# Hybrid decoder block with expert retrieval: both halves of the expert V rows accumulated by TensorE in two lasting PSUM banks

## The reference

```python
h = rmsnorm(x); q, k, v, gb, gc, hc = split(h @ w_in, 6)            # 6 parts of 512 columns
x = x + concat(rmsnorm(stick_breaking_attention(q, k, v)),           # 8 heads of 64
               rmsnorm(gb * conv3(gc * hc))) @ w_out
xn = rmsnorm(x)
# PEER, for each token and each of 8 heads:
s1, s2 = query halves @ keys            # 2 x 128 scores; top 16 of each, then top 16 of the 256 sums
idx, g = 16 expert numbers, softmax of their sums
act = gelu(dot(xn, u_tab[idx]))         # one dot product of 1024 per expert
x = x + sum over the 128 experts of (g * act) * v_tab[idx]
out = rmsnorm(x)
```

## Time and profile before

| | |
|---|---|
| runs | 3486.37, 3487.28, 3492.98 us; median 3487.28 us |
| profiled execution | 3507.52 us, its span 3505.8 us |
| TensorE busy with matmuls | 2478.2 us (71% of the span), 7568 |
| TensorE loading weights | 1334.6 us (38%) |
| VectorE busy | 2666.1 us (76%), 6520 |
| ScalarE, GpSimd busy | 691.0 us (20%), 1359.8 us (39%) |
| DMA | 1213.87 MB, mean 346 GB/s; gathers take 78.5% of 16 engines' span, plain loads and stores 10.4% |
| granted TensorE clock | 0.843 of full speed |
| chunk sums (L1355) start at | 689.3, 1147.6, 1591.2, 1985.8, 2378.9, 2772.3, 3133.3, 3495.1 us |

### The profile page before, as it was taken

How to read it: one execution, slowest core, us unless ns; L and a number is a source line. 1 busy time by engine, 2 the same in 40 slices (tenths; PEclk the granted TensorE clock), 3 DMA queues, 4 the chain that set the end, 5 groups by cost and what they waited for, 6 DMA issues and landing times.

```text
span 3505.8 us, 29116 instructions
## 1 busy us (share of the span) xinstructions
PE 2478.2 (71%) x7568; PEld 1334.6 (38%) x7568; DVE 2666.1 (76%) x6520; ACT 691.0 (20%) x1951; POOL 1359.8 (39%) x1296
## 2 busy tenths in 40 slices
PE   8569985589989785675878787676567555544554
PEld 7447463256545342223544333343223222211221
DVE  1674789865778799896778788689877577777776
ACT  2022311121434111112114332111111111111111
POOL 0132322333334333444444444344444444454443
PEclk9889998799999897898988898798888767776777
DMA  6878797789888997899998999999888899999997
GB/s 216 321 299 324 275 380 289 282 337 355 329 315 331 380 365 303 334 346 365 404 410 338 350 362 382 389 402 369 343 347 338 334 381 383 378 368 371 373 378 301
DMA packets 187117, 1213.87 MB, mean 346 GB/s; under 512 B 20704, under 2 KB 22752, under 8 KB 55520
## 3 DMA queue, kind: packets, MB, share of 16 engines
q0 software_dynamic: 147456, 1073.81, 78.5%
q1 hardware_dynamic: 39520, 138.45, 10.4%
HBM read 1198.54 MB, written 13.63 MB: 346 GB/s over the span
## 4 chain that ended last, share of the span: by engine, by line
PE 34%; DVE 30%; DMA 22%; issue 6%; ACT 5%; POOL 2%; POOLq 0%; DVEq 0%; ACTq 0%; SPq 0%
DMA ring<-in_uv,cur_idx 20%; PE vacc L922 16%; DVE ring L1103 12%; PE bank L960 7%; DVE acc L1134 4%; PE bank L1028 3%; ACT diag L747 3%; POOL ring L710 2%; PE o_ps L926 2%; DMA xn<-in_final_norm_g 1%; PE bank L956 1%; DVE lt L1251 1%; DVE ocT L1261 1%; PE bank L989 1%; PE bank L971 1%
## 5 line engine op out<-in xcount | busy, mean ns | idle before, releaser
L922 PE MATMUL vacc<-ring,diag 128*128 128x512 f32 x2048 | 1281.9, 771 | 968.8 <-ACT diag L747 964.9
L710 POOL DMA_INDIRECT ring<-in_uv,cur_idx x1024 | 1198.1, 1170 | 1191.9 <-PE vacc L922 661.9
L1103 DVE CUSTOM_DVE_ANT_0 ring<-ring,xn 128x1024 f32<-128x1024 f32 x1024 | 1221.0, 1223 | 367.8 <-DMA ring<-in_uv,cur_idx 361.1
L922 PEld LDWEIGHTS vacc<-ring,diag 128*128 128x128 f32 x2048 | 488.6, 250 | 1658.2 <-ACT diag L747 1005.2
L1134 DVE SCALAR_TENSOR_TENSOR acc<-ring,g_w,acc 128x512 f32<-128x512 f32 x832 | 625.6, 752 | 35.2 <-DVE g_w L1126 0.6
L701 POOL COPY cur_idx<-idx 128x4 uint32<-128x4 uint32 (+1 forms) x256 | 159.7, 624 | 924.5 <-DVE acc L1134 706.2
L742 ACT ACTIVATE g_ex<-g_cu 128x4 f32<-128x4 f32 x256 | 52.4, 205 | 2071.8 <-DVE g_cu L1116 2041.0
L747 ACT ACTIVATE diag<-ident,g_w 128x128 f32<-128x128 f32 x1024 | 326.9, 390 | 185.6 <-DVE g_w L1126 181.8
L960 PE MATMUL bank<-hT,wpool 128*128 128x256 f32 (+2 forms) x1280 | 285.3, 382 | 1.4 <-ACT hT L773 1.4
L960 PEld LDWEIGHTS bank<-hT,wpool 128*128 128x128 f32 x1280 | 220.1, 193 | 69.3 <-issue 12.3
L1039 PE MATMUL bank<-hT,wpool 128*128 128x256 f32 (+2 forms) x1024 | 234.2, 384 | 0.7 <-ACT hT L857 0.7
(11 more groups left out here) (129 smaller groups left out, 1813.8 us busy)
## 6 DMA issues: line engine op xcount, KB each, us to landing
wpool<-in_w_in SPq DMA_DIRECT2D x96, 512.0 KB
wpool<-in_peer_wq SPq DMA_DIRECT2D x64, 512.0 KB
wpool<-in_w_out SPq DMA_DIRECT2D x32, 512.0 KB
ring<-in_uv,cur_idx POOLq DMA_INDIRECT x1024, 8.6
xb<-in_x SPq DMA_DIRECT2D x15, 512.0 KB
x_scratch<-xb SPq DMA_DIRECT2D x8, 512.0 KB
xn_scratch<-xb SPq DMA_DIRECT2D x8, 512.0 KB
xn<-xn_scratch SPq DMA_DIRECT2D x8, 512.0 KB
```

What stands on the lines that cost most here:

```text
L710: nc.gpsimd.indirect_dma_start(ring[:, s, :], None, uv, bass.IndirectOffsetOnAxis(ap=cur_idx[:, s:s + 1], axis=0))\
L922: ins = nc.tensor.matmul(vacc[:, :], diag[:, q, s, :], ring[:, q * GROUP + s, D:D + PE_COLS], start=first and s == 0, stop=last and s == G ...
L1103: ins = nc.vector.tensor_tensor_reduce(out=ring[:, s, 0:D], in0=ring[:, s, 0:D], in1=xn[:, c % 2, :], scale=1.0, scalar=0.0, op0=ALU.mult, ...
```

## The change

Every group is now treated as the wide ones were, with a PSUM bank of its own for the second half. `wide_groups`, `is_wide`, `add_rows` and the semaphore `s_vd` are gone. The new bank `vacc2` is taken from the front stages: BANKS falls from 6 to 5. The pool "att" keeps four banks (1 to 4), "mix" has one (0) where it had two, and "all" has five. GpSimd waits for `s_vp` where it waited for `s_vd` before it copies the indices. `final_sum` always has two additions.

```diff
-BANKS = 6
+BANKS = 5
-            choice = {"all": range(BANKS), "att": range(2, BANKS), "mix": range(2)}[pool_of]
+            choice = {"all": range(BANKS), "att": range(1, BANKS), "mix": range(1)}[pool_of]
+        vacc2 = ctx.enter_context(nc.psum_tensor("vacc2", [P, D - PE_COLS], F32))
...
                 if not very_first:
-                    pool.wait_ge(s_vd, used + 1)
+                    pool.wait_ge(s_vp, used + 1)
                 nc.gpsimd.tensor_copy(cur_idx[:, sl], ...)
...
                     if not very_first:
-                        pool.wait_ge(s_vd, used + s % GROUP + 1)
                         pool.wait_ge(s_vp, used + s % GROUP + 1)
...
                 for s in range(GROUP):
-                    ins = nc.tensor.matmul(vacc[:, :], diag[:, q, s, :], ring[:, q * GROUP + s, D:D + PE_COLS], ...)
-                    if wide:
-                        ins = nc.tensor.matmul(o_ps[:, :], diag[:, q, s, :], ring[:, q * GROUP + s, D + PE_COLS:2 * D], ...)
-                    ins.then_inc(s_vp, 1)
+                    nc.tensor.matmul(vacc[:, :], diag[:, q, s, :], ring[:, q * GROUP + s, D:D + PE_COLS], ...)
+                    nc.tensor.matmul(vacc2[:, :], diag[:, q, s, :], ring[:, q * GROUP + s, D + PE_COLS:2 * D],
+                                     ...).then_inc(s_vp, 1)
...
                     weights(G, sl)
-                    if is_wide(c, i, q):
-                        dve.sem_inc(s_vd, GROUP)
-                    else:
-                        add_rows(c, G, q, first)
...
                     dve.wait_ge(s_vp, (c + 1) * SLOTS)
-                    dve.wait_ge(s_vd, (c + 1) * SLOTS)
-                    if c in wide_from:
-                        nc.vector.tensor_tensor(acc[:, c % 2, PE_COLS:D], o_ps[:, :], acc[:, c % 2, PE_COLS:D], ALU.add)
+                    nc.vector.tensor_tensor(acc[:, c % 2, PE_COLS:D], vacc2[:, :], acc[:, c % 2, PE_COLS:D], ALU.add)
```

More of the change, by code:

```diff
@@ L253, in timeline @@
     return out
[L256 to L264, removed]
 def batch_of(c):
@@ L315, in build @@
     line = timeline()
-    wide_from = wide_groups(line)
     phases = [("pe", "turn_keys"), ("act", "store_keys")] + [ph[1:] for ph in line if ph[0] == "front"]
@@ L505, in build @@
         s_gw = sem("s_gw")
-        s_vd = sem("s_vd")
         s_diag = sem("s_diag")
@@ L524, in span @@
             return slice(lc_of(c) * P, (lc_of(c) + 1) * P)
-        def is_wide(c, i, q):
-            return c in wide_from and 2 * i + q >= wide_from[c]
         def gather_line(eng_group, eng_front, me):
@@ L915, in group @@
                     pe.wait_ge(s_fsum, c)
[L916 to L919, removed]
                 pe.wait_ge(s_diag, n * 2 + q + 1)
                 for s in range(GROUP):
-                    ins = nc.tensor.matmul(vacc[:, :], diag[:, q, s, :], ring[:, q * GROUP + s, D:D + PE_COLS],
-                                           start=first and s == 0, stop=last and s == GROUP - 1,
-                                           skip_group_check=True)
-                    if wide:
-                        ins = nc.tensor.matmul(o_ps[:, :], diag[:, q, s, :], ring[:, q * GROUP + s, D + PE_COLS:2 * D],
-                                               start=first_wide and s == 0, stop=last and s == GROUP - 1,
-                                               skip_group_check=True)
-                    ins.then_inc(s_vp, 1)
+                    nc.tensor.matmul(vacc[:, :], diag[:, q, s, :], ring[:, q * GROUP + s, D:D + PE_COLS],
+                                     start=first and s == 0, stop=last and s == GROUP - 1, skip_group_check=True)
+                    nc.tensor.matmul(vacc2[:, :], diag[:, q, s, :], ring[:, q * GROUP + s, D + PE_COLS:2 * D],
+                                     start=first and s == 0, stop=last and s == GROUP - 1,
+                                     skip_group_check=True).then_inc(s_vp, 1)
             def front(name, args):
@@ L997, in front @@
                         pe.wait_ge(s_gain, c)
[L998 to L1002, removed]
                     for i in range(4):
@@ L1126, in weights @@
                 nc.vector.tensor_tensor(g_w[:, sl], g_xg[:, sl], g_re[:, sl], ALU.mult).then_inc(s_gw, 1)
[L1128 to L1136, removed]
             def front(name, args):
@@ L1350, in front @@
                     dve.wait_ge(s_vp, (c + 1) * SLOTS)
-                    dve.wait_ge(s_vd, (c + 1) * SLOTS)
-                    if c in wide_from:
-                        nc.vector.tensor_tensor(acc[:, c % 2, PE_COLS:D], o_ps[:, :], acc[:, c % 2, PE_COLS:D],
-                                                ALU.add)
+                    nc.vector.tensor_tensor(acc[:, c % 2, PE_COLS:D], vacc2[:, :], acc[:, c % 2, PE_COLS:D], ALU.add)
                     nc.vector.tensor_tensor(acc[:, c % 2, 0:PE_COLS], vacc[:, :], acc[:, c % 2, 0:PE_COLS], ALU.add)\
```

## The result

The changed kernel takes 3873.1 us (median of 4 runs, 3870.6 to 3879.3) against 3487.4: ratio 1.109, interval 1.107 to 1.111. It is 386 us slower where 212 were forecast, and lies outside the range. The profiled execution took 3871.3 us, its span 3869.6.

A forecast was written before the change was run, and what follows sets the result against it. No engine is full on average; TensorE, VectorE or DMA bounds it by stretch. Terms 141 - 34 + 30 + 50 + 15 + 10 = 212 us on the median 3487.3 gave about 3700 us, range 3590 to 3810.

The forecast's parts named there:

- three kinds of stretch: Core read in windows: TensorE full, VectorE full with TensorE half idle, or DMA nearly full (chunks 3, 4, 6, 7).
- The lost bank: In the "mix" pool each use waits until the one before was read: plus 50 us, bounds 0 and 100.
- the first wait: Second part of `out_proj(c, 0)` waits for VectorE's read of the first, over 23 group parts: 48 us.
- The tail: Chunks 6 and 7: two matmuls and the index copy delay the next gather: plus 15 us, bounds minus 15 and plus 95.
- The chain's own step: Chunks 6 and 7: the first gather of a group starts 1.2 us later with TensorE warm, 2.9 us cold.
- the price of a group: Chunks 6 and 7: 0.6 or 1.5 us each, less what the loop can spare, taken as 0.25 us x 64.
- VectorE's relief: Four stretches where VectorE is full get shorter without its adds: minus 34 us, bounds minus 58 and 0.
- Stretches where TensorE is full: 224 to 540, 733 to 1156 and 1203 to 1322 us: added matmuls cost 39, 85 and 17, together 141 us.
- Chunks 3 and 4: TensorE becomes as full as DMA and some idle time stays: plus 30 us together, bounds 0 and 120.
- Groups already wide: In the 48 groups wide before, only the index copy moves: plus 10 us, bounds 0 and 29.
- stalls feed on each other: Rival: a still TensorE frees no ring places, DMA runs dry, TensorE works at half clock: 3809 us, chance 0.12.
- weight-load rule: Judges TensorE by weight-load share, so matmuls would fit in chunk 1; points to the rival of 3377 us, chance 0.05.

The follow-up runs named there:

- with six banks: The changed kernel with the front's six banks kept, TensorE summing both halves into one bank, so they are not kept apart: 3768.6 us, ratio 1.076.

## Why the prediction was wrong

The direction and the three kinds of stretch held, and each mechanism named is seen at work. What failed are the sizes of terms, nearly all to the same side; in the largest a wait was taken for partly harmless.

- **The lost bank: the step that failed.** The forecast counted 48 us for the first wait and 20 to 30 for the others, and then took 50, because part would fall into slack. It costs 118 alone and 104 on top of the matmuls. In the change the count of the stalls was right: 61.0 us in front of second parts and 12.5 in front of `turn_xn`, together 73.5 where 68 to 78 were counted. With VectorE's adds still there they are longer, 92.2 and 20.3 us. The discount to 50 was wrong: the group matmuls behind the wait hold ring places, so the gathers stop (DMA at 0.35 and 0.01 in chunk 4 above), and the whole wait is paid. The forecast also had no term for the clock: the second parts took 76.8 us where they took 57.5 before, 19 us more (6.36 us for 3.60 in the worst). Stalls and cold matmuls make 93 of the 103 us between the profiles of the change with five and with six banks.
- **The tail.** 15 us forecast, 42 in the change, 53 with six banks. The chain's own step was right (2.9 us for the cold case, 2.85 measured). The failed step is the price of a group: the forecast took 0.6 to 1.5 us less "about 1 us" to spare, hence 0.25, and with six banks each of the 63 groups up to 7:31 took 0.83 more. How much of that is the spare time and how much the clock isn't separated. The bound of 95 held.
- **VectorE's relief.** 34 us forecast. In its four stretches it is 27 with nobody adding the second half, but with TensorE's matmuls 9 (1.9, none, 6.2 and 1.1). Why is only argued: TensorE's slots may come free later there, so that VectorE waits for gathers instead.
- **Stretches where TensorE is full.** 39, 85 and 17 us forecast. With six banks 53 in the first; 91.5 in chunk 1 from group 3 on, where 85 stood; 12 in the eight groups of the third, 2:3 to 2:11. The first took off 22 us for a warmer clock and for idle time used; only 8 came. 6 us more came in groups 0 to 2 of chunk 1.
- **Chunks 3 and 4.** 30 forecast, 45 measured with six banks, and some 5 to 10 more if the profile of before was long in chunk 3, as the table's introduction says. Within the bounds of 0 and 120.
- **Groups already wide.** 10 forecast, 12 measured (chunks 0, 2 and 5 with six banks: -1.2, +4.8, +8.0).

With six banks the profiles differ by 261 us where 162 were forecast; of the 99 between them 38 are the tail and 25 the relief. The bank adds 104 to 118 for 50. Of the rivals, "stalls feed on each other" was nearest (3809). Its 100 us for the bank are what was measured, and the dry DMA and the half clock behind a stall are those that it names; its 75 for the tail are too much (42 to 53), and it kept the forecast's other terms, which were too small.

On the weight-load rule of the Trainium skill ("Perfetto Trace Analysis", Identifying the Most-Contended Engine): the run with six banks speaks against it for this kernel. With 65% (0:4 to 0:22) and 55% (chunk 1) of its time in weight loads TensorE had no room: each group took 3.0 and 3.2 us longer for the 3.43 us given to it. The section names MFU, the achieved share of the peak arithmetic rate, beside the weight-load share; the forecast used only the latter, and no MFU was worked out here.

## What to carry to other kernels

Moving work to an engine is worth what the receiving engine has to spare in each stretch of the kernel, not on average: 626 us less on VectorE were worth 42 at most, and the matmuls of all second halves took 306 (3768.6 against 3462.2). A PSUM bank taken from a pool of two turns double buffering into strict alternation of two in-order engines, and the time of every instruction listed between writer and reader is then paid by whatever queues behind. Count these instructions, and before you discount them as slack, ask what the waiting engine holds: here it held the ring, and the gathers stopped. Work that only frees a buffer later, or a small copy that moves behind a release, cost time in chunks 6 and 7, where DMA was at 0.96.

## What was not expected of the hardware

TensorE came back cold from a stall of 6.8 us: the granted clock was 0.57 in the 6.3 us behind it, and four matmuls 128x512 took 6.36 us instead of 3.60. The stall cost 2.8 us more than its length. And a copy of four indices on GpSimd, 0.2 to 0.9 us long, put 20 us on each of the chunks 6 and 7 (31.4 against 10.5, and 26.0 against 8.0) by standing in front of the first of four gathers, while TensorE had two matmuls to a slot. With one matmul to a slot the same late copy cost 5.6 and 2.3.
